# FFN up projection by Strassen's seven sub-products per tile pair, and a down projection that reads its gated input back from DRAM

## The reference

```python
def conv_gated_ffn(h, w_up, conv_w, conv_b, w_down):      # h 1024 x 1024, w_up 1024 x 8192, w_down 4096 x 1024
    S = h.shape[1]
    u = h @ w_up
    u_pad = jnp.pad(u, ((0, 0), (CONV_WIDTH - 1, 0), (0, 0)))          # CONV_WIDTH = 3, along the tokens
    u = conv_b + sum(conv_w[j] * u_pad[:, j:j + S] for j in range(CONV_WIDTH))
    gate, val = jnp.split(u, 2, axis=-1)
    return (jax.nn.gelu(gate, approximate=True) * val) @ w_down

        f = conv_gated_ffn(rms_norm(x, norm_ffn_pre[l]), w_ffn_up[l], conv_w[l], conv_b[l], w_ffn_down[l])
        x = x + rms_norm(f, norm_ffn_post[l])
```

## Time and profile before

| | us |
|---|---|
| three runs | 2530.18, 2530.26, 2538.0 |
| median | 2530.26 |
| span of the profiled execution, first to last instruction | 2528.9 |
| TensorE busy | 2433.1 (96%) |
| VectorE / ScalarE / GpSimd busy | 1202.0 / 737.0 / 953.2 |
| mean granted TensorE clock | 0.984 |

### The profile page before, as it was taken

One profiled execution on the slowest core, in us unless ns is written; L12 is line 12 of the kernel. 1 busy time (PEld: TensorE's weight loads), 2 busy tenths in 40 slices (PEclk: granted clock), 3 DMA queues, 4 the chain that ended last, 5 costly groups with the idle time before them and its releaser, 6 DMA issues.

```text
span 2528.9 us, 45291 instructions
## 1 busy us (share of the span) xinstructions
PE 2433.1 (96%) x17978; PEld 1945.9 (77%) x17978; DVE 1202.0 (48%) x1653; ACT 737.0 (29%) x1138; POOL 953.2 (38%) x536
## 2 busy tenths in 40 slices
PE   8999989999989999999999999999999999998798
PEld 5777779996868888888888888878778777773367
DVE  4476775545454421443143312333553266656564
ACT  3233542223332200221022101221253234557641
POOL 3322100003634433444334433346676355530045
PEclk9999989999989999999999999999999999999899
DMA  4311000002432211221122111123421111121033
GB/s 149 80 34 34 26 8 4 4 4 76 130 103 68 73 58 58 75 68 57 58 66 75 59 50 50 50 74 121 164 92 59 38 51 47 51 81 73 1 112 121
DMA packets 52214, 164.44 MB, mean 65 GB/s; under 512 B 5336, under 2 KB 7640, under 8 KB 51928
## 3 DMA queue, kind: packets, MB, share of 16 engines
q1 hardware_dynamic: 29088, 105.92, 13.2%
q10 hardware_dynamic: 22968, 56.31, 6.7%
HBM read 141.76 MB, written 20.45 MB: 64 GB/s over the span
## 4 chain that ended last, share of the span: by engine, by line
PE 87%; DVE 7%; ACT 3%; issue 1%; POOL 1%; DVEq 0%; DMA 0%; ACTq 0%; POOLq 0%
PE ps L557 55%; PE ps L1125 5%; PE ps L653 5%; PE ps L1148 2%; ACT ab L116 2%; PE ps L833 1%; PE ps L823 1%; PE ps L602 1%; DVE proj L116 1%; PE ps L830 1%; PE ps L567 1%; DVE x_lo L116 1%; PE ps L665 1%; PE ps L787 1%; PE ps L1228 1%
## 5 line engine op out<-in xcount | busy, mean ns | idle before, releaser
L451 POOL TENSOR_TENSOR w_hi<-w_raw,small 128x1024 fp32r<-128x1024 f32 x194 | 375.2, 1934 | 1301.1 <-PE ps L557 945.0
L557 PE MATMUL ps<-x_hi,w_hi 128*128 128x512 f32 x1600 | 536.3, 394 | 12.9 <-DVE x_lo L116 9.8
L557 PE MATMUL ps<-x_hi,w_lo 128*128 128x512 f32 x1600 | 529.5, 390 | 0.0
L557 PE MATMUL ps<-x_lo,w_hi 128*128 128x512 f32 x1600 | 529.5, 390 | 0.0
L454 POOL TENSOR_TENSOR w_lo<-w_raw,w_hi 128x1024 fp32r<-128x1024 f32 x194 | 473.8, 2442 | 15.2
L557 PEld LDWEIGHTS ps<-x_hi,w_hi 128*128 128x128 f32 x1600 | 300.2, 188 | 85.9 <-DVE x_lo L116 15.8
L557 PEld LDWEIGHTS ps<-x_hi,w_lo 128*128 128x128 f32 x1600 | 301.1, 188 | 63.4
L557 PEld LDWEIGHTS ps<-x_lo,w_hi 128*128 128x128 f32 x1600 | 301.3, 188 | 61.1 <-issue 0.2
L116 DVE SCALAR_TENSOR_TENSOR cv<-ps,cst,cv 128x1023 f32<-128x1023 f32 (+2 forms) x66 | 82.5, 1250 | 256.8 <-ACT cv L116 251.3
L557 PE MATMUL ps<-f_hi,w_hi 128*128 128x512 f32 x512 | 170.0, 393 | 2.0 <-DVE f_lo L116 2.0
L557 PE MATMUL ps<-f_hi,w_lo 128*128 128x512 f32 x512 | 168.9, 391 | 0.0
(11 more groups left out here) (308 smaller groups left out, 3783.4 us busy)
## 6 DMA issues: line engine op xcount, KB each, us to landing
w_raw<-wall SPq DMA_DIRECT2D x194, 512.0 KB, 3.5
ada_w<-wada ACTq DMA_DIRECT2D x24, 512.0 KB, 3.6
fill_spill<-stage ACTq DMA_DIRECT2D x24, 256.0 KB, 2.0
x_in<-xT ACTq DMA_DIRECT2D x8, 512.0 KB, 8.8
x<-xT ACTq DMA_DIRECT2D x8, 512.0 KB, 4.2
x_spill<-x ACTq DMA_DIRECT2D x16, 256.0 KB, 2.0
x_in<-x_spill ACTq DMA_DIRECT2D x16, 256.0 KB, 3.4
x_spill<-x ACTq DMA_DIRECT2D x2, 2048.0 KB, 9.1
```

The costliest lines, as they stand in the source:

```text
L451: nc.gpsimd.tensor_tensor(w_hi[:, u, :, :], w_raw[:, u, :, :], sm["one"].unsqueeze(2).to_broadcast([P, KT, P]), ALU.mult).then_inc(S("w_hi ...
L557: last = mm(ps[:, 2 * u + h, :], w[:, u, k, :], x[:, k, h * 512:(h + 1) * 512], start=(k == 0 and w is w_hi and x is hi), stop=(k == KT - ...
```

## The change

Up tiles 0 and 1 (the first pair) are done as before. Each of the other 31 pairs is one 2 x 2 block product: the gate tile and the value tile are the two weight columns, the chunks 0 to 3 and 4 to 7 the two halves of the sum, the two token halves the other side. Instead of eight block products of 12 matmuls (4 chunks x 3) there are seven. For that

- GpSimd makes sums and differences of weight halves (128 x 512 each) and their `lo` parts: per pair four sums, five `slot_low` and one `gate_low` of 128 x 1024. ScalarE makes the `hi` parts (`slot_high`, `gate_high`), which GpSimd made before.
- The four sums of the input's blocks (`t_hi`, `t_lo`) are made once, before and during pair 1, by GpSimd, ScalarE and DVE. The normed input `y1` is now in SBUF, not in PSUM.
- The seven products go to four PSUM banks per pair (two sets of four in turn). ScalarE copies two of them out, DVE makes the five block sums (`c11`, `c22` twice, `c12`, `c21`, 128 x 512) into `c_gate` and `c_val` in SBUF, and the convolution then reads SBUF.
- The gated product of each pair is written to DRAM. There is no `f_hi`/`f_lo` any more in this phase. The slice of `w_ada` is summed up in SBUF.

When all pairs are done, a second phase does the down projection: 2 token halves x 2 groups of four output tiles, each in 16 steps over two gated chunks. A step loads 512 KB of weights in pieces of 1 KB and 512 KB of gated products in pieces of 2 KB, GpSimd splits the weights, ScalarE and DVE split the gated products (`f_high`, `f_low`, 128 x 1024), and TensorE does 24 matmuls into four banks. Adding to `f_acc` is gone; the norm and residual work is placed between the steps.

```diff
+            def first_sums(p, q, turn):            # GpSimd, per pair
+                pool.wait_ge(*later(f"a_in{q}", 16 * turn))
+                pool.wait_ge(*later(f"v_in{q}", 16 * turn))
+                tt_p(scr[:, q, 0, :, :], v_raw[:, q, 0:4, :], v_raw[:, q, 4:8, :], ALU.add).then_inc(later("s_sum")[0], 1)
+                tt_p(scr[:, q, 1, :, :], w_raw[:, q, 0:4, :], v_raw[:, q, 0:4, :], ALU.subtract).then_inc(later("s_sum")[0], 1)
...
+                    first_sums(p, q, i + u)
+                    gate_low(p, q)
+                    slot_low(p, 0, scr[:, q, 0, :, :])
+                    second_sum(p, q)
+                    slot_low(p, 1, scr[:, q, 0, :, :])
+                    fourth_sum(p, q)
+                    slot_low(p, 2, scr[:, q, 1, :, :])
+                    slot_low(p, 3, scr[:, q, 0, :, :])
+                    slot_low(p, 4, v_raw[:, q, 4:8, :])
...
+            def up_pair(p, q, first=False):        # TensorE
+                pe.wait_ge(*later("a_lo", p))
+                if not first:
+                    pe.wait_ge(*later("st_c", 5 * p - 9))
+                product(q, 0, 0, fresh=True)
+                product(q, 1, 1, fresh=True)
+                pe.wait_ge(*later("s_lo", 5 * p - 4))
+                product(q, 2, 2, fresh=True, across=0 if first else None)
+                pe.wait_ge(*later("s_lo", 5 * p - 3))
+                pe.wait_ge(*later("p1_cp", p))
+                product(q, 3, 0, across=4 if first else None)
+                pe.wait_ge(*later("s_lo", 5 * p - 2))
+                product(q, 4, 3, fresh=True, across=8 if first else None)
+                pe.wait_ge(*later("s_lo", 5 * p - 1))
+                pe.wait_ge(*later("st_c", 5 * p - 3))
+                product(q, 5, 2)
+                pe.wait_ge(*later("s_lo", 5 * p))
+                pe.wait_ge(*later("st_c", 5 * p - 2))
+                product(q, 6, 3, across=12 if first else None)
...
+            def down_step(n):                      # TensorE, 64 steps
+                u, dg, j = n % 2, n // N_STEP % 2, n % N_STEP
+                pe.wait_ge(S("w_split"), G_DOWN + n + 1)
+                pe.wait_ge(S("f_lo_done"), n + 1)
...
-                copy(x_hi[:, k, hc(h)], scaled_bank(h, k)).then_inc(S("x_hi_done"), 1)
+                copy(x_hi[:, k, hc(h)], y1[:, k, hc(h)]).then_inc(S("x_hi_done"), 1)
...
+            def up_step(p, q, turn, ada=None, last=False):     # ScalarE, per pair
...
+                second_out(p, q)
+                slot_high(p + 1, 1, scr[:, 1 - q, 0, :, :])
+                slot_high(p + 1, 2, scr[:, 1 - q, 1, :, :])
+                slot_high(p + 1, 3, scr[:, 1 - q, 0, :, :])
+                gate_conv(p)
+                slot_high(p + 1, 4, v_raw[:, 1 - q, 4:8, :])
+                gate_gelu(p)
+                val_conv(p)
+                first_out(p + 1, 1 - q)
+                if not last:
+                    gate_high(p + 2, q, turn)
+                    slot_high(p + 2, 0, scr[:, q, 0, :, :])
+                store(p)
...
+            def taps(dst, src, col):               # DVE; src is c_gate or c_val, in SBUF
+                stt(dst[:, 1:], src[:, 0:T - 1], par("conv_w")[:, bass.ds(64 + col, 1)], dst[:, 1:], ALU.mult, ALU.add)
+                return stt(dst[:, 2:], src[:, 0:T - 2], par("conv_w")[:, bass.ds(col, 1)], dst[:, 2:], ALU.mult, ALU.add)
...
+            def f_low(n):
+                dve.wait_ge(S("f_hi_done"), n + 1)
+                tt(f_part(f_lo, n), f_part(f_raw, n), f_part(f_hi, n).bitcast(F32), ALU.subtract).then_inc(S("f_lo_done"), 1)
...
+            def up_step(p, q, ada=None):           # DVE, per pair
+                c22(p, q)
+                if ada is not None:
+                    n, k = ada
+                    dve.wait_ge(S("load0"), 16 * n + 32)
+                    stt(ada_sum[:, :], ada_w[:, :], sm["silu_c"][:, bass.ds(k, 1)], ada_sum[:, :], ALU.mult, ALU.add)\
+                        .then_inc(S("ada_acc"), 1)
+                c12(p, q)
+                gate_taps(p)
+                c21(p, q)
+                val_taps(p)
+                c11(p + 1, 1 - q)
+                gated_product(p)
```

More of the change, by code:

```diff
@@ new lines, in product @@
+            def product(q, i, b, fresh=False, across=None):
+                hi, lo = moving[i]
+                w1, w2 = (w_hi[:, q, 4 * i:4 * i + 4, :], w_lo[:, q, 4 * i:4 * i + 4, :]) if i < 2 else (slot_hi[i - 2], slot_lo[i - 2])
+                for k in range(4):
+                    if across is not None:
+                        pe.wait_ge(*later("t_lo", across + k + 1))
+                    mm(up_bank(q, b), w1[:, k, :], hi[:, k, :], start=(fresh and k == 0), stop=False, skip_group_check=True)
+                    mm(up_bank(q, b), w1[:, k, :], lo[:, k, :], start=False, stop=False, skip_group_check=True)
+                    last = mm(up_bank(q, b), w2[:, k, :], hi[:, k, :], start=False, stop=(k == 3), skip_group_check=True)
+                last.then_inc(later("st_mm")[0], 1)
@@ L1023, in head_tile @@
+            pe.wait_ge(S("x_lo_done"), 40)
+            for n in range(3 * N_STEP, 4 * N_STEP):
+                down_step(n)
+            pe.wait_ge(*later("down_cp", 12))
             def head_tile(h, k, k0=0, k1=KT):
@@ L1612, in _ @@
+            slot_high(1, 0, scr[:, 0, 0, :, :], first=True)
             for k in range(KT):
@@ L1725, in _ @@
             head_evict(0, 0)
-            half_root("a", 3)
             head_evict(0, 1)
```

717 lines of the change are left out of this document (472 added, 245 removed).

## The result

The changed kernel takes 2613.95 us, the median of four runs (2610.16 to 2618.32), against 2533.58 (2530.18 to 2538.0) for the kernel before in the same comparison: a ratio of 1.032, 95% interval 1.030 to 1.035. Forecast were 2577 us and a range of 2525 to 2640. 4.8 us of the 85 stand there at 655 us already, where both kernels have done the same work.

What follows compares the result with a forecast made beforehand. The prediction took TensorE alone to bound the kernel before, in the FFN. Pairs +18, pair 1 and input sums +17, down steps +10 and phase change 2 gave +47; with span 2528.9 and 1.4 to the median, 2577 us, range 2525 to 2640.

Steps and rivals of the forecast that it cites:

- Twelve matmuls fewer, 19.0 us for TensorE: Pairs 2 to 32: 84 instead of 96 matmuls each, TensorE alone needing 19.0 us per pair, 84.3 us removed in all.
- DVE and GpSimd hold each other where DVE reads two SBUF operands: In each pair, such operations exclude each other for the whole instruction: 20.3 us exclusive time, 21.5 with a w_ada slice.
- The ring of 17.1 us plus 5 in waits, 22.7 and 21.2 per pair: Chain of waits from one pair's sixth product to the next's: 22.7 us with a w_ada slice, 21.2 without.
- the sum of the pairs: Pairs 2 to 31 together: +22 us for those with a w_ada slice, -4 without, +18 in all.
- the upper bound: Per pair, one whole us above the time taken, for an added wait from ScalarE's fixed order and TensorE's lower clock.
- my upper rival: Pairs a full 1.3 us longer (24.0, 22.5) from the lower clock and ScalarE's order: 2634 us, chance 0.20.
- Pair 1 and the start, +17: Making the input sums ends pair 1 about 15 us late and pair 2 another 2: +17, bounds +8 and +27.
- Down steps, +10 by w_lo and f_low taking turns: Down projection: the weight split comes 1.0 us late, half of the excess shows, 64 x 0.15 = +10, bounds 0 and +25.
- The part after, 0: From the last down matmul to the kernel's end: no change in time, 0 us.
- DMA, hidden: Down steps: 1 MB loaded per 5.6 us step uses about 0.6 of the queues, so it adds nothing.
- The rival in which the exclusion costs little: In the pairs, TensorE binds at 19.0 us: about 2458 us, chance 0.05.
- the perfectly packed one: In the pairs, DVE and GpSimd exclude each other without idle time, 20.6 and 19.3 us: 2509 us, chance 0.10.

Runs made afterwards that it cites:

- e1: Changed kernel with all ten GpSimd operations of a pair, in pairs 2 to 31, cut to 8 of each 128 columns (computation incomplete); 2535.44 us, ratio 1.001.
- e5: e4 with DVE's w_ada slice and the wait for its load moved from behind c22 to behind c21; 2517.52 us, ratio 0.9945.
- e11: Changed kernel with only the gate weights' low part, in pairs 2 to 31, cut to 8 of each 128 columns (computation incomplete); 2570.55 us, one run.
- e2: Changed kernel with the four blocks of c kept in PSUM, so taps read one SBUF operand, no operation fewer; 2557.56 us, ratio 1.010.
- e4: e2 and e3 together: c in PSUM, and ScalarE's store and ada_w load behind the copy of u2; 2547.31 us, ratio 1.006.
- e3: Changed kernel with ScalarE's store of the gated product and the ada_w load issued behind the copy of u2; 2596.29 us, ratio 1.025.
- e12: e5 with down-phase one-column products spread, the head's half sums moved later, and steps 2 and 33 reordered; 2486.71 us, ratio 0.983.
- e10: Changed kernel with only the down phase's one-column products spread and the head's four half sums moved later; 2591.31 us, ratio 1.023.

## Why the prediction was right, step by step

- **Twelve matmuls fewer, 19.0 us for TensorE**: right. e1 and e5 have pairs of 19.04 us where nothing is waited for.
- **DVE and GpSimd hold each other where DVE reads two SBUF operands, and the change moves four taps and the w_ada sum there**: right and shown, from GpSimd's side (e1, e11) and, with no operation changed but its address, from DVE's (e2). The size was too large. The taps should have had means of about 2 us; one tap in four met an operation and took 2.06, three took 1.28, a mean of 1.48. I had four waits of 1.0 and one of 1; the trace has one tap, the product and the w_ada sum held, for about 0.8 to 1.1 us each, and GpSimd's delays by them (w_lo 3.04 us, for "about 2.6 or more").
- **The ring of 17.1 us plus 5 in waits, 22.7 and 21.2 per pair**: the sum of the pairs, +17 against +18, was right, but by luck, since its parts were wrong both ways. An ordinary pair was 22.20 us, not 22.7, and pairs 25 to 30 had a mean of 21.3, for 21.2. Pairs 9 and 17 took 27.9 and 27.5: there the memset waits for the store of ada_sum, which I had not costed. Inside an ordinary pair the holds of DVE are 1.9 us of the ring (tap 0.8, product 1.1), not 5. From the end of c22's first sum to c12 it is 4.7 us, where I had 3.1: in one pair the sixth product runs at the lower clock, which I had only in the upper bound, in the next DVE waits 1.5 us for ada_w's load and is then held in its slice. From the product's end to c22 it is 1.8 to 2.25 us, where I had 0.9: ScalarE issues the store and the load of ada_w before it copies u2. These three, 1.9, 1.6 and 1.1, are 4.6 of the 5.1 us over 17.1. TensorE was busy 90% there, not 85%; 19.04 of 22.20 is 86%, and the rest is matmuls at the lower clock.
- **What the ring is**: of the 3.2 us that a pair had above 19.04, the address of the operands alone gave back 1.8 (e2) and the place of the w_ada slice, with its load, 1.1 behind it (e4 to e5). e3 does not settle what the order on ScalarE alone is worth, since its 1.6 us came back as a wait for the load. So my upper rival (a longer ring by the lower clock and ScalarE's order) had the right two additions, and the holds, which I had too large, left room for them.
- **Pair 1 and the start, +17**: right in its main part. Pair 1 was to end 15 us late and last some 38; it lasted 37.3, 15.6 over the 21.75 before. The change made its start 3.6 us late, where I had 2 for x_lo. The other 4.8 of the +24 are the scatter of executions. What I had not costed stands in pair 2: the load that waits for pair 0's store.
- **Down steps, +10 by w_lo and f_low taking turns**: mechanism and size were right. w_lo took 3136 ns and f_low 1942 in the down phase. Between the bursts, in steps 16 to 30 and 46 to 61, the steps come 5.59 us apart in the changed kernel and in e12 (5.6 was forecast), and w_lo ends 0.1 to 0.5 us before the next step. e12, with the same turns, has a down phase of 373.3 us, 7.9 over the 365.4 of before. The term failed in its sentence "where the norm's operations lie between, a little more": bursts of one-column products, four copies ahead of a low part, and low parts behind the last product cost 25.6 us (398.9 less 373.3), 14.8 of which e10 recovered in the changed kernel itself.
- **The part after, 0**: it was +10.4. The four sums that before were spread over the down tiles now stood together behind four copies. e10 took 4.5 of it back, e12 8.2 (749.7 less 741.5), each by one trace in a part that scatters by some 4 us.
- **DMA, hidden**: right for the down steps' loads. The loads that did bind are v_raw's and ada_w's, which have a store before them.

The rival in which the exclusion costs little is refuted; the perfectly packed one (20.6 and 19.3) too, as ordinary pairs were 22.20.
